# Last down pass by column groups with a per-token norm in row layout, gathers of eight tokens, input norm by halves

## The reference

```python
def rms_norm(x, g):
    xf = x.astype(jnp.float32)
    y = xf * lax.rsqrt(jnp.mean(xf * xf, axis=-1, keepdims=True) + EPS)
    return (y * g.astype(jnp.float32)).astype(x.dtype)
...
def decoder_layer(x, pos0, mem_k, mem_v, ckv_past, kr_past, C0, n0, m0, p):
    y, ckv, kr, C, n, m = hybrid_mixer(rms_norm(x, p['g_pre_mix']), pos0, ckv_past, kr_past, C0, n0, m0, p)
    x = x + rms_norm(y, p['g_post_mix'])
    x = x + rms_norm(memory_attention(rms_norm(x, p['g_pre_mem']), mem_k, mem_v, p), p['g_post_mem'])
    x = x + rms_norm(swiglu_ffn(rms_norm(x, p['g_pre_ffn']), p), p['g_post_ffn'])
    return x, ckv, kr, C, n, m
...
        ckv_past = cache_ckv[layer, page_table].reshape(Bs, past_len, KV_LORA)
        kr_past = cache_krope[layer, page_table].reshape(Bs, past_len, QK_ROPE)
```

## Time and profile before

| | |
|---|---|
| median of three runs | 2445.48 us (2444.03 to 2446.78) |
| profiled execution, its own time | 2449.44 us |
| span of its trace | 2447.6 us |
| mean granted clock of TensorE | 0.971 of 2.4 GHz |
| busy: PE, DVE, ACT, POOL | 2265.7 (93%), 1013.3 (41%), 810.7 (33%), 410.8 (17%) us |
| chain that ended last, by engine | PE 74%, DVE 9%, POOL 6%, ACT 5%, issue 4%, DMA 1% |

### The profile page before, as it was taken

How to read it: one execution, slowest core, us unless ns; L and a number is a source line. 1 busy time by engine, 2 the same in 40 slices (tenths; PEclk the granted TensorE clock), 3 DMA queues, 4 the chain that set the end, 5 groups by cost and what they waited for, 6 DMA issues and landing times.

```text
span 2447.6 us, 38563 instructions
## 1 busy us (share of the span) xinstructions
PE 2265.7 (93%) x16195; PEld 2008.0 (82%) x16195; DVE 1013.3 (41%) x1797; ACT 810.7 (33%) x1392; POOL 410.8 (17%) x464
## 2 busy tenths in 40 slices
PE   4999989999998999888999798979999999899993
PEld 4999989997544676665899676859999999899993
DVE  3452133334376654444451846471111111255556
ACT  5221222222344444444243334441111111144542
POOL 0000011101200277774043510200000000000000
PEclk9999989999999999999899999999999999999997
DMA  4122233332200277775431242121111111101121
GB/s 132 44 87 87 87 108 113 111 92 99 85 1 1 111 233 233 235 235 155 147 130 35 69 158 83 35 79 51 43 45 49 43 51 43 56 26 45 47 93 69
DMA packets 186495, 223.38 MB, mean 91 GB/s; under 512 B 17977, under 2 KB 149510, under 8 KB 185622
## 3 DMA queue, kind: packets, MB, share of 16 engines
q1 hardware_dynamic: 155254, 114.33, 15.2%
q0 software_dynamic: 31136, 107.56, 13.7%
HBM read 191.88 MB, written 29.98 MB: 91 GB/s over the span
## 4 chain that ended last, share of the span: by engine, by line
PE 74%; DVE 9%; POOL 6%; ACT 5%; issue 4%; DMA 1%; POOLq 0%; ACTq 0%; SPq 0%; DVEq 0%
PE ps L1535 26%; PE ps L1097 18%; PE ps L1828 10%; PE ps L1585 2%; POOL mem_high L990 2%; POOL mem_low L990 2%; POOL mem_high L991 1%; POOL mem_low L991 1%; PE ps L1445 1%; PE ps L1261 1%; PE ps L1734 1%; PE ps L1374 1%; PE ps L1379 1%; PE ps L1475 1%; ACT mem_low L2045 1%
## 5 line engine op out<-in xcount | busy, mean ns | idle before, releaser
L1097 PE MATMUL ps<-stream_first,early_first 128*128 128x344 f32 x912 | 298.7, 328 | 4.3 <-DVE H_short L2472 3.0
L1097 PE MATMUL ps<-H_short,early_first 128*128 128x344 f32 x912 | 294.2, 323 | 0.0
L1097 PE MATMUL ps<-stream_first,ring_short 128*128 128x344 f32 x912 | 293.8, 322 | 0.0
L1535 PE MATMUL ps<-stream_first,sel_short 128*128 128x344 f32 x1152 | 252.1, 323 | 8.0 <-DVE H_short L2861 3.6
L1535 PE MATMUL ps<-H_short,sel_short 128*128 128x344 f32 x1152 | 251.2, 322 | 1.6 <-DVE ring_short L2867 1.6
L1535 PE MATMUL ps<-stream_first,ring_short 128*128 128x344 f32 x1056 | 228.8, 320 | 0.0
L1535 PEld LDWEIGHTS ps<-stream_first,sel_short 128*128 128x128 f32 x1152 | 195.3, 188 | 13.2 <-DVE H_short L2861 5.8
L1535 PEld LDWEIGHTS ps<-H_short,sel_short 128*128 128x128 f32 x1152 | 196.9, 190 | 2.1 <-DVE ring_short L2867 2.0
L2867 DVE TENSOR_TENSOR ring_short<-ring_raw,sel_short 128x1024 fp32r<-128x1024 f32 (+1 forms) x64 | 70.0, 1093 | 296.3 <-ACT sel_short L2116 296.3
L1097 PEld LDWEIGHTS ps<-stream_first,early_first 128*128 128x128 f32 x912 | 174.3, 191 | 13.1 <-ACT mem_high L1953 6.1
L1535 PEld LDWEIGHTS ps<-stream_first,ring_short 128*128 128x128 f32 x1056 | 177.5, 188 | 0.0
(11 more groups left out here) (532 smaller groups left out, 4283.9 us busy)
## 6 DMA issues: line engine op xcount, KB each, us to landing
ring_raw<-w_ffn_in SPq DMA_DIRECT2D x44, 512.0 KB, 3.7
ring_raw<-w_in SPq DMA_DIRECT2D x37, 512.0 KB, 3.8
ring_raw<-w_ffn_out SPq DMA_DIRECT2D x16, 704.0 KB, 4.7
branch_gates<-mem_high POOLq DMA_DIRECT2D x16, 516.0 KB, 4.6
chunks_apart<-mem_high POOLq DMA_DIRECT2D x12, 516.0 KB, 2.9
mem_high<-chunks_apart POOLq DMA_DIRECT2D x8, 768.0 KB, 5.8
mem_low<-branch_gates SPq DMA_DIRECT2D x2, 2064.0 KB
mem_high<-branch_gates SPq DMA_DIRECT2D x1, 4128.0 KB
```

Source lines behind the costliest of these rows:

```text
L1097: mm = pe.matmul(ps[:, bank, 0:TN], w[:, k], x[:, k, j * TN:(j + 1) * TN], start=(k == 0 and q == 0), stop=(k == KT - 1 and q == 2))
L1535: mm = pe.matmul(ps[:, s + j, 0:TN], w[:, k], x[k][:, j * TN:(j + 1) * TN], start=(k == 0 and q == 0), stop=(k == kts - 1 and q == 2))
```

## The change

Four things, independent of each other in the code.

*Gathers.* A row of the index holds 8 tokens instead of 4, and one DMA fills two groups: 8 KB of latents and 1 KB of rope keys a partition, two pairs of DMAs a unit. The index is page x 16 + (partition mod 16) and takes two pages a quadrant, so it is made in two steps on DVE; the attention does not depend on the order of the tokens.

*Input norm.* The first four token tiles get their variances and root before the second four are squared. The scaling by the root moves from ACT to DVE (4 tiles ahead of the first split, 4 and the samples after it). The gains are loaded on ACT's queue; on SP the first four weights stand ahead of the constants. The transposes use a ring of five banks, and the first third of product 0 stands ahead of tiles 13 to 15.

*Last down group.* Groups 0 to 2 stay as they were, with a scaled copy (gain `g_post_ffn`) of each output tile behind its square. Group 3 runs over the columns in three parts, 384, 384 and 264 wide, each over all 22 hidden tiles, with four buffers.

*End.* No channel-layout norm: the column sums come out as one column a token tile (128 x 1), so variance, reciprocal and root are on 3 columns (`result_sum`, `part_variance`, `part_root`). For each half token tile TensorE transposes 4 tiles of the output and 4 of the residual into two banks (`result_turn`), ACT copies the residual to its place (`residual_copy`) and DVE adds the output times the token's factor (`result`). Twelve of the 18 halves are done inside the parts 1 and 2, at the tiles that `HALVES` names. The residual returns in three column pieces.

```diff
@@ SP @@
+            residual_in(0)
+            residual_in(1)
+            for i in range(3):
+                result_out(i)
+            residual_in(2)
+            for i in range(3, TT):
+                result_out(i)
...
@@ POOL: gather @@
-                for g in range(GROUPS):
-                    at = bass.IndirectOffsetOnAxis(ap=idxu[s][:, g:g + 1], axis=0)
-                    pool.indirect_dma_start(ukv[s][:, g].rearrange("p r c -> p (r c)"), None, ckv_rows, at).then_inc(kv_in[s], 16)
-                    pool.indirect_dma_start(ukr[s][:, g], None, kr_rows, at).then_inc(kv_in[s], 16)
+                for h in range(2):
+                    at = bass.IndirectOffsetOnAxis(ap=idxu[s][:, h:h + 1], axis=0)
+                    pool.indirect_dma_start(ukv[s][:, 2 * h:2 * h + 2].rearrange("p g r c -> p (g r c)"), None, ckv_rows, at).then_inc(kv_in[s], 16)
+                    pool.indirect_dma_start(ukr[s][:, 2 * h:2 * h + 2].rearrange("p g x -> p (g x)"), None, kr_rows, at).then_inc(kv_in[s], 16)
...
@@ TensorE: input @@
+            for n in range(13):
+                turn_input(n)
+            pe.wait_ge(weights_rest_ok, 1)
+            pe.wait_ge(split_rest_ok, KT)
+            third(0, 0, 0)
+            for n in range(13, 2 * KT):
+                turn_input(n)
...
@@ TensorE: end @@
+        HALVES = {(1, 8): 0, (1, 10): 1, (1, 13): 2, (1, 15): 3, (1, 18): 4, (1, 20): 5,
+                  (2, 8): 6, (2, 10): 7, (2, 13): 8, (2, 15): 9, (2, 18): 10, (2, 20): 11}
...
+            def result_turn(n):
+
+                i, h = n // 2, n % 2
+                j, b = min(i // 3, 2), 2 + 2 * (n % 2)
+                rows = P if i < TT else NB
+                pe.wait_ge(h_back, 16 * (j + 1))
+                pe.wait_ge(evac_act, 4 + FT + 2 * LAST + 2 * (j + 1))
+                pe.wait_ge(out_scaled, 2 * LAST)
+                if n >= 2:
+                    pe.wait_ge(result_copied_dve, n - 1)
+                for x, src in enumerate((A, H2)):
+                    for k in range(4):
+                        mm = pe.transpose(ps[0:rows, b + x, k * P:(k + 1) * P], src[:, 4 * h + k, i * P:i * P + rows], ident)
                 mm.then_inc(result_turned, 1)
...
+                        for n, (wt, x) in enumerate(((hi, hid_hi_part[t % 4]), (hi, hid_lo_part[t % 4]), (lo, hid_hi_part[t % 4]))):
+                            mm = pe.matmul(ps[:, LAST_BANK[j] + m, 0:w], wt[:, kk], x[:, 0:w],
+                                           start=(k == 0 and n == 0), stop=(k == FT - 1 and n == 2))
+                    mm.then_inc(tile_used, 1)
+                    if j and k == 5:
+                        result_sum(j - 1)
+                    if (j, k) in HALVES:
+                        result_turn(HALVES[j, k])
...
@@ ACT: groups 0 to 2, then the last @@
                 act.activation(sqb6[m], A[:, 2 * g + m], ACT.Square).then_inc(nrm_sq, 1)
+                act.wait_ge(nrm_sq, g * 2 + (squares_before(2) + m + 1))
+                act.activation(A[:, 2 * g + m], A[:, 2 * g + m], ACT.Copy,
+                               scale=gains[:, G_POSTFFN + 2 * g + m:G_POSTFFN + 2 * g + m + 1]).then_inc(out_scaled, 1)
...
+            for j in range(NP3):
+                for k in range(FT):
+                    if j == 0 and k < 2:
+                        down_evac(LAST - 1, k)
+                    part_first(j, k)
+                    if (j, k - 1) in HALVES:
+                        residual_copy(HALVES[j, k - 1])
...
+                    if j and k < 2:
+                        part_evac(j - 1, k)
+                    if j and k == 8:
+                        part_root(j - 1)
...
@@ DVE: end @@
+            def result(n):
+                i, h = n // 2, n % 2
+                b, rows = 2 + 2 * (n % 2), P if i < TT else NB
+                dve.wait_ge(nrm_rstd, norm_no(2) + min(i // 3, 2))
+                dve.wait_ge(result_copied_act, n + 1)
+                to = Y[:, 4 * h:4 * h + 4, i * P:(i + 1) * P] if i < TT else ysn.rearrange("p (k c) -> p k c", k=KT)[:, 4 * h:4 * h + 4]
+                dve.scalar_tensor_tensor(out=to, in0=ps[0:rows, b].rearrange("p (k c) -> p k c", k=4), scalar=row_rs[0:rows, i:i + 1], in1=to,
+                                         op0=ALU.mult, op1=ALU.add).then_inc(result_copied_dve, 1)
```

309 lines of the change are left out of this document (198 added, 111 removed).

## The result

The changed kernel takes **2433.19 us** (median of 5, 2430.40 to 2435.18) against 2444.03 for the kernel before on the same chip (median of 5, 2441.08 to 2446.78): a ratio of 0.9946, 95% interval 0.9928 to 0.9965, so 9 to 18 us less. The forecast was 2424 in a range of 2414 to 2438: right sign, inside the range, about half of the gain. The two profiled spans differ by more than the medians, 2447.6 against 2431.2, since the profiled execution of before lies 5.4 us above its median and the other at its own.

A forecast was written before the change was run, and what follows sets the result against it. TensorE, 93% busy, was taken as the bound, slowed by POOL's gathers in later decode units. Savings 15.2 + 5.2 + 2.2 - 1.2 = 21.4 us took the profiled 2449.44 to 2428.0; less 3.96 above the median, 2424, range 2414 to 2438.

The forecast's parts named there:

- units 9 to 30 run at 9.49: Decode: with four gathers a unit, TensorE's 9.49 us sets the pace; 22 x 0.69 = 15.2 us saved.
- waits on its own chain and stays: Decode's tail after unit 31: waits on its own chain, so no time is gained or lost there.
- The 13 slow matmuls: Input, first third of the first product: 13 of 24 matmuls at the lower clock, 0.29 us each.
- lowest case, "3.5": Input: only 3.5 us saved if the clock has fallen by 44 and 13 matmuls are slow again.
- two weight pieces ... cost 2.2: Last down group, first column group: splitting two weight pieces on ACT, with rests on DVE, costs 2.2 us.
- the handovers: Last down group: TensorE idles behind turned half tiles, 1.25 us each in second column group, 1.44 in third, five times each.
- The scaled copies: Down groups 0 and 1: scaled copies behind output tiles' squares make splits about 0.3 late four times, 1.2 us lost.
- Clock, in part: Rival: a third to half of column groups 1 and 2 at 1.2 GHz, 13 to 18 us more, 2440; chance 0.15.
- Clock, throughout: Rival: column groups 1 and 2 run wholly at 1.2 GHz, 38 us more, 2462, slower; chance 0.06.
- The gathers don't bind less: Rival: 8 KB rows land no faster than 235 GB/s, decode keeps 10.1 us a unit, 2439; chance 0.10.
- Handovers hidden: Rival: ACT and DVE run further ahead, half of 16 us of waits in groups 1 and 2 goes, 2416; chance 0.11.

The follow-up runs named there:

- the gathers alone: The kernel before with only the gathers of eight tokens changed: 2439.43 us, ratio 0.9973 to the kernel before.
- the latents alone: The kernel before with units 4 to 31 gathering only latents in 4 KB rows, their rope keys left out: 2435.07 us in one run.
- the second execution of before: The kernel before, unchanged, run and profiled a second time: 2444.96 us, span 2443.2.

## Why the prediction was right or wrong

**Decode: mechanism right, size wrong.** Forecast 15.2, found 11.1 - 2.1 = 9.0 in the profiled pair. That POOL bound units 9 to 28 and TensorE takes over at 9.49 is shown three ways: the waits of both engines, the gathers alone, the latents alone. The step that failed is "units 9 to 30 run at 9.49". I took 10.18 us from an average up to unit 30, and two units at the end of that stretch were not of its kind: unit 29 and unit 30 stood 11.57 and 11.56 apart, the others 10.05. Unit 30 was held not by a gather at all but by the copies behind a split, for 2.40 us; at unit 29 the wait for the DMA, 2.03, covered the same split up to 0.31. With the DMA on time the split shows, 2.40 us at each unit, and so neither unit gets shorter. That the split is the cause is shown by its move (stage 4 from 55.1 to 45.5). That both get longer, by 1.3 and 1.2, is the lower clock behind the wait, for which the forecast had no term. I put an end of its own ("waits on its own chain and stays") only behind unit 31 and counted units 29 and 30 among those that the gathers bound. Two rows more, the value products of units 28 and 29, would have told that the average was mixed.

**Input: the sum right, by two deviations that cancel.** Forecast 5.2, found 5.6 in the pair; over all executions stage 1 is 577.2 to 581.1 without this part and 572.7 to 573.8 with it as it was written. Steps on the way: four scalings in 2.74 for 3.0, the first third at 33.95 for 34.8, the second at 42.02 for 44.0, where the kernel before starts it at 49.14. That is 7.1 us earlier. The 13 slow matmuls that I put into the first third did not come, so the splits behind it ended 2 us earlier; eleven or twelve matmuls at the lower clock came behind the wait ahead of the second instead and took 1.5 back. The working had the lower clock there only in its lowest case, "3.5"; that the two deviations cancel is luck. The early third got credit in my working that it does not deserve.

**Last group: total close, two terms off in opposite ways.** From the third group's end to the end of the span I forecast 115.3, and it is 2431.2 - 2318.0 (the row at 2318.80 less its 0.81) = 113.2. That these are 2 us apart owes something to luck, for the terms are further off than their sum. The first column group took 32.3 for 27.7: the term "two weight pieces ... cost 2.2" missed that the pieces are asked for only at the group's start, and that thirds of a tile reach the splits sooner than whole tiles did. This is shown by the move of the splits, 6.6 us. In the other direction, the handovers cost 0.97 and 1.15 for 1.25 and 1.44; that their place in the orders of ACT and DVE was the cause, as the working said, is shown by their move, 11.5 us. The second column group was 35.6 for 37.8, the third 30.9 for 32.4, and what follows the last matmul 14.5 for 17.4. The scaled copies in groups 0 to 2 cost about 0.5, not 1.2 (stage 6 falls by 0.6, where the shorter start of the last group, 0.81 of idle for 1.93, would give 1.1).

**The baseline.** The forecast subtracted 21.4 from the profiled time and then the 3.96 by which that execution exceeded its median, so it took for granted that the excess stays. The changed kernel's profile shows 5.0 less gain than forecast (16.4); the other 4 are that excess, which the second execution of before did not have. Most of it lay in stages with drops of the clock, 2.1 us in stage 1, which the change touches, and 2.7 in stages 2 and 5, which it does not. Against that second execution, which ran near the median, the changed kernel's is 12.0 us shorter: stages 1, 3, 6 and 7 gain 18.1, stage 4 loses 1.6, and stages 2 and 5, with the same program, lose 4.7. So about half of the 9.4 us that are missing from the forecast there lies in stages that the change leaves alone; stage 5 differs that much between executions of one program.

**The rivals.** *Clock, in part*: not in the place where I put it. In the column groups the granted clock is 1.00 over 35.5 and 29.7 us, with eight transposes in each pair of tiles and a wait behind them; the Trainium skill's statement in TensorE: Matmul & The Clock Gate, Part 4: PE-mode transpose, that a transpose does not count as busy the way a matmul does, would make this rival's time by my reading, and the trace does not bear it out here. The clock did fall behind single waits, at 42, 1120, 1133 and 2326. *Clock, throughout*: no. *The gathers don't bind less*: no, 9.49 a unit, at 252 GB/s from 926 to 1110 us. *Handovers hidden*: they were not, but they can be, which was the most useful of the four to have priced: half of 16 us by its text, 11.5 by the run that moves them.

## What to carry to other kernels

An average rate over a loop's units holds units of different kinds; before a gain is multiplied by their number, look at the spacing of each, at the last ones above all. When a loop's step gets shorter, everything that was placed by step number (a weight's split after part 2) moves earlier in time while the transfer it waits for does not; check each such place against the landing. And work that is put between a turn and the next split on an in-order engine is paid by TensorE: one tile behind its turn it cost a wait each time here, three tiles behind, with four buffers, ten of the waits went.

## What was not expected of the hardware

- An indirect DMA on POOL costs the same 0.93 to 0.96 us with its 0.30 of dispatch whether its rows hold 512 B, 1 KB, 4 KB or 8 KB; for POOL's time in these runs only their number counted.
- Single-column memsets on POOL last 0.10 us each in the rows of the start, but begin 0.03 apart, and 44 in a row take 1.51, 0.034 each.
- The granted clock falls behind single waits of TensorE, 2.13, 2.40 and 3.72 us here, and then stands at the 1.2 GHz level, for 3 to 7 us in these places. The same wait does not always do it. The turns of the last latents, before and in the changed kernel, behind the same 2.40 us of idle:

```profile
1148.54 1.94 PE L1445 MATMUL ps<-mem_low 128*128 128x128 f32 x16 [2.40 <-DVE mem_high L2797]
```

took 1.94 us at 1.00 there, and 3.29 in the row at 1120.20 above. In the second execution of the kernel before the clock did fall behind this wait:

```profile
1145.28 2.46 PE L1445 MATMUL ps<-mem_low 128*128 128x128 f32 x16 [2.40 <-DVE mem_high L2797]
```

Over all executions it does not look like chance: with the splits in their old place and four gathers a unit, units 29 and 30 took 12.6 to 13.0 us in each of seven; with eight gathers they took 11.56 or 11.57 in four, but for this unit 30, which took 12.09. From the last scores to the value product TensorE did only turns in both kernels, so the wait alone is not shown to be the cause. What decides it stays open, and with it the 952 to 958 us of stage 5.
